# Prompt attention of a hybrid decoder step: the gate and the softmax sum move from the probability rows into a scaled identity

## The reference

```python
def masked_softmax(s, mask, axes=-1):
    ...
    e = jnp.where(mask, jnp.exp(s - m), 0.0)
    return e / jnp.maximum(jnp.sum(e, axis=axes, keepdims=True), 1e-30)

def nsa_combine(gn, o_cmp, o_slc, o_win):
    return (gn[:, :, 0, :, :, None] * o_cmp + gn[:, :, 1, :, :, None] * o_slc
            + gn[:, :, 2, :, :, None] * o_win)
```

## Time and profile before

| what | value |
|---|---|
| median of 3 runs | 1881.05 us (1879.68 to 1882.05) |
| the profiled execution's own time | 1884.05 us |
| its span in the trace | 1882.2 us |
| TensorE busy (share of the span) | 1724.1 us (92%) |
| VectorE, ScalarE, GpSimd busy | 546.0, 335.9, 454.5 us |
| prompt attention, first to last matmul | 370.25 to 489.37 us |
| first matmul of the stage behind it | 491.13 us |
| first matmuls of the expert loop | 845.17 us |

### The profile page before, as it was taken

How to read it: one execution, slowest core, us unless ns; L and a number is a source line. 1 busy time by engine, 2 the same in 40 slices (tenths; PEclk the granted TensorE clock), 3 DMA queues, 4 the chain that set the end, 5 groups by cost and what they waited for, 6 DMA issues and landing times.

```text
span 1882.2 us, 40022 instructions
## 1 busy us (share of the span) xinstructions
PE 1724.1 (92%) x16122; PEld 965.1 (51%) x16122; DVE 546.0 (29%) x1347; ACT 335.9 (18%) x736; POOL 454.5 (24%) x522
## 2 busy tenths in 40 slices
PE   7997876688799999969999999999999999999992
PEld 3545762444588886533556673444443434343431
DVE  2222014266111111372323232323232322222226
ACT  3232222255200000111111111111111111111110
POOL 1113547377100001411222212121222222222220
PEclk9997976789799999969999999999999999999996
DMA  8207877540431103057999999999999999999986
GB/s 303 102 31 224 308 199 224 168 175 1 151 116 56 52 27 117 23 210 307 424 425 413 425 423 413 424 426 417 425 414 414 424 426 421 413 421 420 420 363 244
DMA packets 84179, 535.93 MB, mean 285 GB/s; under 512 B 19601, under 2 KB 43633, under 8 KB 71154
## 3 DMA queue, kind: packets, MB, share of 16 engines
q1 hardware_dynamic: 63065, 493.83, 65.2%
q0 software_dynamic: 14544, 32.03, 5.0%
q10 hardware_dynamic: 6512, 9.33, 1.4%
HBM read 518.72 MB, written 28.39 MB: 291 GB/s over the span
## 4 chain that ended last, share of the span: by engine, by line
PE 53%; DVE 1%; DMA 0%; issue 0%; POOLq 0%; POOL 0%; ACT 0%; SPq 0%
PE psum L2874 35%; PE psum L2900 18%; DVE arena L2856 1%; PE psum L2884 0%; DVE arena L2864 0%; DMA arena<-y_of 0%; DMA y_of<-arena 0%; DMA arena<-scr_h,arena 0%; DVE arena L2807 0%; POOL arena L2744 0%; POOLq L2675 0%; ACT arena L2793 0%; POOLq L2748 0%; POOLq L2744 0%; POOLq L2750 0%
## 5 line engine op out<-in xcount | busy, mean ns | idle before, releaser
L2874 PE MATMUL psum<-arena 128*32 128x512 f32 x6144 | 668.0, 592 | 2.8 <-issue 2.8
L2874 PEld LDWEIGHTS psum<-arena 128*32 128x32 f32 x6144 | 234.6, 108 | 416.8 <-issue 413.2
L2900 PE MATMUL psum<-arena 128*32 128x256 f32 x6144 | 344.8, 378 | 0.0
L2900 PEld LDWEIGHTS psum<-arena 128*32 128x32 f32 x6144 | 235.9, 109 | 110.1 <-issue 10.4
L2829 DVE TENSOR_TENSOR arena<-psum,arena 128x512 f32<-128x512 f32 x96 | 66.5, 692 | 592.1 <-PE psum L2874 592.1
L2761 POOL DMA_INDIRECT y_of<-arena x96 | 96.9, 1010 | 471.6 <-ACT arena L2793 471.6
L2505 PE MATMUL psum<-arena 128*128 128x272 f32 x768 | 184.0, 398 | 1.8 <-PEq L231 1.8
L2505 PEld LDWEIGHTS psum<-arena 128*128 128x128 f32 x768 | 147.7, 192 | 35.9 <-issue 3.4
L2789 ACT ACTIVATE arena<-arena 128x256 f32<-128x256 f32 x96 | 40.1, 418 | 610.1 <-DVE arena L2831 610.1
L2740 POOL DMA_INDIRECT arena<-scr_h,arena x96 | 99.5, 1036 | 49.3 <-POOL arena L2736 28.5
L799 PE MATMUL psum<-arena 128*128 128x512 f32 (+1 forms) x256 | 90.1, 510 | 0.2 <-DVE arena L660 0.2
(11 more groups left out here) (364 smaller groups left out, 1473.5 us busy)
## 6 DMA issues: line engine op xcount, KB each, us to landing
arena<-in_w_gu SPq DMA_DIRECT2D x64, 4096.0 KB, 14.6
arena<-in_w_down SPq DMA_DIRECT2D x32, 4096.0 KB, 14.1
arena<-in_w_gb SPq DMA_DIRECT2D x24, 512.0 KB, 3.5
arena<-y_of SPq DMA_DIRECT2D x8, 1024.0 KB, 13.7
arena<-in_cache_cmp SPq DMA_DIRECT2D x62, 128.0 KB
arena<-in_cache_slc SPq DMA_DIRECT2D x60, 128.0 KB, 3.0
arena<-in_w_tok SPq DMA_DIRECT2D x3, 2048.0 KB, 10.5
arena<-in_x_all SPq DMA_DIRECT2D x8, 512.0 KB, 11.3
```

The source lines that it names most:

```text
L2874: mm = pe.matmul(gu_bank(g)[32 * j:32 * j + 32].rearrange("p (h n) -> p h n", h=2), xgT[:, g, 32 * k:32 * k + 32], gu_w(slot)[:, part, :, ...
L2900: mm = pe.matmul(dn_half(g)[32 * j:32 * j + 32], actT[:, g, 32 * k:32 * k + 32], dn_w(slot)[:, part, 256 * j:256 * j + 256], start=(k == 0 ...
```

## The change

A buffer `scaled_ident` is added, one 128 x 128 matrix for each head and each of the three groups in flight. For selected and local groups GpSimd no longer multiplies the rows of `probs`. It writes the identity, each row multiplied by that query's number, into the matrix of the head. TensorE then turns the unscaled rows by a true product with that matrix instead of a transpose with the identity: the rows are again the stationary operand and the scaled identity is streamed. Ahead of a group's first step GpSimd waits until the turns of the group three back are done, since their matrices are overwritten. Memory and compressed groups are as they were: rows scaled, then transposed.

```diff
--- before.py
+++ after.py
@@ -1797,6 +1797,7 @@
         peak = take(2, 8)
         total = take(2, 8)
         scale_of = take(2, 8)
+        scaled_ident = take(RING, 8, 128)
         assert cursor[0] <= w_gb_at
         cursor[0] = w_gb_at
         w_gb = take(6, KD, 128)
@@ -1877,10 +1878,10 @@
                         pool.tensor_tensor(compact(n), compact(n), c.rearrange("q (g p) -> q g p", g=2).unsqueeze(3)
                                            .to_broadcast([128, 2, 4, NCMP_P]), ALU.mult).then_inc(a_pr, 1)
                     else:
-                        w = 128 * (t + 1)
+                        if p == 0 and n >= RING:
+                            pool.wait_ge(a_tp, 2 * v_last[n - RING] + 2)
                         for g in range(2):
-                            rows = probs[:, n % RING, 4 * g + p, 0:w]
-                            ins = pool.tensor_scalar(rows, rows, c[:, g:g + 1], None, ALU.mult)
+                            ins = pool.tensor_scalar(scaled_ident[:, n % RING, 4 * g + p], ident, c[:, g:g + 1], None, ALU.mult)
                         ins.then_inc(a_pr, 1)
 
             @block.scalar
@@ -2069,7 +2070,11 @@
                             else:
                                 src = probs[:, n % RING, 4 * g + k, 128 * a:128 * a + 128]
                             rows = NCMP_P if kind == CMP else 128
-                            mm = pe.transpose(bank(4 + g)[0:rows, 128 * k:128 * k + 128], src, ident)
+                            out = bank(4 + g)[0:rows, 128 * k:128 * k + 128]
+                            if kind in (SLC, WIN):
+                                mm = pe.matmul(out, src, scaled_ident[:, n % RING, 4 * g + k], start=True, stop=True)
+                            else:
+                                mm = pe.transpose(out, src, ident)
                         mm.then_inc(a_tp, 1)
 
                 def values(j):
```

## The result

| | before | after |
|---|---|---|
| median of 6 runs each | 1882.05 us (1879.68 to 1884.58) | 1890.99 us (1889.42 to 1894.67) |
| the profiled execution's own time | 1884.05 us | 1889.51 us |
| prompt attention, its first matmul to the next stage's first | 120.88 us | 129.67 us |

The ratio is 1.0051, with a 95% interval of 1.0037 to 1.0065: slower by 7 to 12 us. The forecast was 1890.0 in a range of 1884.0 to 1897.0, and slower by more than 0.2%. A second measurement of both kernels gave 1.0044 (1.003 to 1.0057).

What follows compares the result with a forecast made beforehand. Prompt attention lies on the path, bound by TensorE in most slots and by GpSimd at a few places; 18.2 (turns) - 7.35 (waits) - 2.0 - 0.8 + 0.9 (clock) = +8.95 us, forecast median 1890.0 us, range 1884.0 to 1897.0.

Steps and rivals of the forecast that it cites:

- GpSimd's gain, 7.35 us: Prompt attention, selected and local groups: 128-column scaling steps shorten TensorE's waits for GpSimd, saving 7.35 us together.
- The turns, 20 x 0.91 = 18.2 us: Selected and local branches: each of 20 turns becomes 16 loads and 16 matmuls, 1.94 us instead of 1.03, +18.2 us.
- the price of a half: One of a turn's 16 matmuls: 113 ns, from streaming in proportion to columns, above the load's 106.
- A step could even cost twice as much and stay hidden.: GpSimd's scaling step of 1.21 us: against a slot of nearly 4 us, even double the cost would stay hidden.
- The clock: Half-clock stretches after TensorE's longer waits: 2.0 and 0.8 us come back, the last turn costs 0.9 more.
- The second stretch: After the wait before 445.55: some 3 us at the lower clock lose 1.5; half, 0.8 us, is taken back.
- The stretch after the wait of tile 1: Half-clock work after the wait before 468.10: left as it was, no term in the sum.
- The last turn's 0.9: Last turn, at 484.55: runs at the lower clock with twice the work, 0.9 us more than already counted.
- The sum: Whole kernel: 18.2 - 7.35 - 2.0 - 0.8 + 0.9 = +8.95 us.
- The clock stays up: Rival: real products keep TensorE's upper clock through the stage, so half-speed stretches go; +1.15 us, 1882.2 us, chance 0.12.
- The loads are not hidden: Rival: each half pays load and stream, 219 ns; +43 us, 1924 us; mild form 1897; chance 0.06.
- Faster: Rival: a product's halves share one load, so turns stay at 1.03 us; 10.1 us won, 1870.9 us, chance 0.06.

Runs made afterwards that it cites:

- the two variants: Changed kernel with each product streaming 64 of 128 columns, or loading 64 of 128 query columns; turn 1.93 us and 1.85 us against 1.98.
- the second execution: The unaltered changed kernel measured and profiled again; ratio 1.0044 to the kernel before, changed part of the stage 102.47 us where the first profile had 104.71.
- the TensorE part alone: Kernel before, with selected and local rows still scaled in place but turned by a true product with the plain identity; ratio 1.0106, +20.0 us.
- the GpSimd part alone: Changed kernel, but TensorE still transposes with the plain identity, so selected and local rows stay unscaled; ratio 0.9939 to the kernel before, -11.5 us.

## Why the prediction was right, point by point

- **GpSimd's gain, 7.35 us.** Measured 15.2 - 7.9 = 7.3. Place by place: 3.7 for the 3.9 at 404, 1.4 for 1.4, 1.27 for 1.25, 0.64 for 0.6, 0.2 for 0.2 at the short one, nothing in tile 0. This step held.
- **The turns, 20 x 0.91 = 18.2 us.** The two records for each product came as said, and nothing absorbed their time. The size was 20 x 0.95 = 19.0. The part that failed is the price of a half: 113 ns was taken from the stream in proportion to its columns, and I held the load to be covered at 106. Measured were 119, and by the two variants the load weighs more in them than the stream. That the error cost only 0.8 us in the sum is luck: 6 ns too little in 320 halves are 1.9 us, and the 0.13 us that the turn was given beyond its sixteen halves came out at 0.08, which took 1.1 back.
- **"A step could even cost twice as much and stay hidden."** Wrong. It is hidden in the dense slots, but ahead of six of the eight groups' first turns TensorE then waits for the last step (the four waits shown above, and 2.17 at 455.65 and 0.95 at 470.81); doubled, it cost 20.5 us. The sum does not use this sentence.
- **The clock.** The 2.0 us after the first wait came back as said. The second stretch went altogether: 1.5 where I took 0.8. The stretch after the wait of tile 1, which I left alone, got dearer: at 469.26 the turn took 3.71 us to the next start, the queries 0.73, the next turn 2.81, that is 1.73 + 0.31 + 0.83 = 2.9 us over full clock, against 1.6 before, since real products have twice the work to do at half speed. The last turn's 0.9 was right in this execution (3.78 against 1.97) and nearly nothing in the second one of the same kernel (2.98). So the places of the clock terms were right and their sizes in part luck.
- **The sum.** 19.0 - 7.3 - 2.0 - 1.5 + 1.3 + 0.9 = +10.4, against 10.06 measured in the changed part of the stage and the predicted 8.95. Costs were taken 2.1 too low (0.8 for the turns, 1.3 in tile 1) and a gain 0.7 too low (the second stretch), so a third of the error cancelled. In the second execution the same part is +7.8: there 19.0 for the turns, -7.3 for the waits and -3.7 for the clock give 8.0. The prediction had the clock at -1.9, the first execution at -1.5. The prediction lies between the two, and so do the ratios' +8.3 to +9.6. The turns and the waits were right by their mechanism; that the total fits to about 1 us owes something to luck.
- **The rivals.** *The clock stays up*: it fell after the last waits with real products too, and in the kernel with the TensorE part alone after the same 5.28 us. After a wait of 1.97 us it stayed up in the GpSimd part alone, which has transposes (turn of 1.09 at 455.89), and fell in the changed kernel (3.78 at 469.26); after 2.03 it fell with transposes in the kernel before, and stayed up with products in the TensorE part alone (2.05 at 454.66). The kind of instruction alone does not decide. The Trainium skill (TensorE: Matmul & The Clock Gate, Part 4) says that transposes count differently as activity; the runs show no such difference that holds from one execution to the next, and the earlier trace rows has 1.00 over 12 us with transposes in them. *The loads are not hidden*: 119, not 219. *Faster*: the GpSimd part alone gave about what that rival gives, -11.5 for -10.1, so the price of the product is where it failed.

## What to carry to other kernels

A float32 transpose on TensorE is recorded as one load and one stream, a float32 product as two of each; to fold a scale into the turning matrix costs as much again as the turn, so it pays only where the engine that did the scaling holds TensorE up by more than that. Here the first selected group was tried alone and pays; by the prices above the local group of tile 2 comes out about even (three turns, 2.9 us, for 1.3 of wait and 1.5 of half clock), and the other six lose. Before work is moved to the engine that is busy in nearly every slot, look for one that is not: VectorE took half of the rows for 0.3 to 0.5 us per step, which gave -9.8 us, the same within the noise as the -11.5 of GpSimd's part of the change alone. And price a wait with the work that runs at half clock behind it.

## What the runs showed of the hardware

- Eight float32 transposes of 128 x 128 take 1.03 us, eight float32 products of that size 1.98. With 128 weight columns the products' halves are 119 ns apart for 128 streamed columns and 115 for 64, while in the earlier trace rows those with 32 streamed columns came 106 ns apart. With 64 weight columns and 128 streamed they are 110 to 113. Where the 9 to 13 ns above the 106 come from was not tried.
- A row of 128x384 float32 costs GpSimd 1.47 us when VectorE begins its own multiplication 0.05 us before it:

```profile
422.74 0.42 DVE L2011 TENSOR_SCALAR arena<-arena 128x384 f32<-128x384 f32 x1
422.79 1.47 POOL L1882 TENSOR_SCALAR arena<-arena 128x384 f32<-128x384 f32 x1 [1.44 <-DVE arena L2008]
```

and 1.25 when VectorE begins 0.34 us after it:

```profile
421.97 1.25 POOL L1884 TENSOR_SCALAR arena<-arena 128x384 f32<-128x384 f32 x1 [1.62 <-DVE arena L2010]
...
422.31 0.45 DVE L2020 TENSOR_SCALAR arena<-arena 128x384 f32<-128x384 f32 x1
```

The Trainium skill (GPSIMD Engine Reference, Key points) says that GpSimd shares its SBUF interfaces with VectorE and contends with VectorE's instructions in a two-port mode or with two SBUF inputs. The first pair fits that, if VectorE's multiplication is of that kind, which no row shows. In the second the two overlap as well and GpSimd is not slowed; there VectorE's is the longer one (0.45, and 483 ns on average against 421). So the runs do not settle what the 0.22 us are.
- Of the waits ahead of a turn of the two branches, those from 1.87 to 2.95 us were followed by turns at the lower clock in some kernels and not in others, with transposes and with products alike, and also differently in two executions of one kernel (the turn behind 2.94 us: 3.78 and 2.98). No turn right behind a wait of 1.56 us or less was slowed, and every one behind a wait of 3.3 us or more was (3.34, 3.37, 3.93, 5.28 twice, 7.08).
